# Prompt attention of a two-layer decoder trunk: softmax normalised on the finished output instead of on the probabilities

## What is computed

```python
def block(args):                      # one block of 128 queries
    qi, ci, pi = args
    s = jnp.einsum('bqhd,bkhd->bhqk', qi, k).astype(F32) * scale
    s = s + ci[..., None] - ckt[:, :, None, :]
    s = jnp.where(k_pos[None, :] <= pi[:, None], s, MASK_VALUE)
    p = jax.nn.softmax(s, axis=-1).astype(v.dtype)
    return jnp.einsum('bhqk,bkhd->bqhd', p, v)
```

## Time and profile before

| | us |
|---|---|
| median of three runs | 2067.57 (2066.80 to 2072.34) |
| the profiled execution, time | 2069.26 |
| the profiled execution, span of the trace | 2066.1 |
| TensorE busy in the span | 1897.4 (92%) |
| VectorE busy in the span | 920.6 (45%) |
| ScalarE busy in the span | 673.6 (33%) |
| first score product of prompt attention to the end of its last output copy | 1070.93 to 1169.36: 98.4 |

### The profile page before, as it was taken

The page is one execution under the profiler, slowest core; times in us unless marked ns, Lnnn a source line. Parts: engine busy times, 40 slices in busy tenths (PEclk is TensorE's granted clock), DMA queues, the critical chain, the costliest instruction groups (busy, mean ns, idle before and its releaser), DMA issues. The chain is left out here.

```text
span 2066.1 us, 39402 instructions
## 1 busy us (share of the span) xinstructions
PE 1897.4 (92%) x16433; PEld 1726.6 (84%) x16433; DVE 920.6 (45%) x1393; ACT 673.6 (33%) x1047; POOL 572.9 (28%) x263
## 2 busy tenths in 40 slices
PE   4999997999999999998979779888887999999998
PEld 4899996899999999998967546555546999999998
DVE  3767756235555400234448744433332255555100
ACT  4455464232222222344326424333332422222111
POOL 1333231233333433333335100000002333333332
PEclk9999998999999999999979979999997999999999
DMA  4232331222222322222231389999992222223222
GB/s 104 73 104 77 86 95 45 72 73 84 85 86 84 87 85 71 64 69 62 72 115 46 91 320 377 390 388 388 389 379 85 78 82 82 82 82 90 85 85 74
DMA packets 288994, 272.91 MB, mean 132 GB/s; under 512 B 19953, under 2 KB 249426, under 8 KB 288178
## 3 DMA queue, kind: packets, MB, share of 16 engines
q1 hardware_dynamic: 288674, 269.35, 40.3%
q0 software_dynamic: 144, 1.05, 0.2%
HBM read 252.09 MB, written 14.08 MB: 129 GB/s over the span
## 5 line engine op out<-in xcount | busy, mean ns | idle before, releaser
L1713 POOL TENSOR_TENSOR b_wl<-b_wraw,b_wh 128x1024 fp32r<-128x1024 f32 (+1 forms) x68 | 177.4, 2609 | 714.5 <-ACT b_wh L1651 714.5
L1713 POOL TENSOR_TENSOR a_wl<-a_wraw,a_wh 128x1024 fp32r<-128x1024 f32 (+2 forms) x91 | 243.3, 2674 | 433.3 <-ACT a_wh L1651 433.3
L1609 PE MATMUL ps<-xh,a_wh 128*128 128x288 f32 x1104 | 242.9, 302 | 0.0
L1609 PE MATMUL ps<-xl,a_wh 128*128 128x288 f32 x1104 | 238.0, 297 | 0.0
L1609 PE MATMUL ps<-xh,a_wl 128*128 128x288 f32 x1104 | 237.4, 297 | 0.0
L1651 ACT ACTIVATE a_wh<-a_wraw 128x1024 fp32r<-128x1024 f32 (+2 forms) x91 | 100.5, 1104 | 354.4 <-PE ps L1609 348.9
L1201 PEld LDWEIGHTS ps<-ident,sa_kp 128*128 128x128 f32 x1024 | 125.4, 154 | 83.9 <-DMA sa_kp<-in_cache_k 50.2
L1201 PE MATMUL ps<-ident,sa_kp 128*128 128x128 f32 x1024 | 141.8, 298 | 53.5 <-DMA sa_kp<-in_cache_k 44.3
L1651 ACT ACTIVATE b_wh<-b_wraw 128x1024 fp32r<-128x1024 f32 (+1 forms) x68 | 77.1, 1134 | 346.3 <-PE ps L1609 319.1
L1728 DVE TENSOR_TENSOR xT<-xT,ps 128x576 f32<-128x576 f32 x32 | 24.1, 754 | 355.3 <-PE ps L1609 355.3
L1609 PEld LDWEIGHTS ps<-xh,a_wh 128*128 128x128 f32 x1104 | 179.1, 188 | 3.0 <-issue 0.2
(11 more groups left out here) (296 smaller groups left out, 3872.6 us busy)
## 6 DMA issues: line engine op xcount, KB each, us to landing
sa_kp<-in_cache_k SPq DMA_DIRECT2D x128, 512.0 KB, 10.1
sa_vp<-in_cache_v SPq DMA_DIRECT2D x128, 512.0 KB, 14.5
a_wraw<-in_w_gate_up SPq DMA_DIRECT2D x44, 512.0 KB, 3.9
b_wraw<-in_w_gate_up SPq DMA_DIRECT2D x44, 512.0 KB, 3.9
a_wraw<-in_a_w_in SPq DMA_DIRECT2D x32, 512.0 KB, 4.1
a_wraw<-in_w_down SPq DMA_DIRECT2D x16, 704.0 KB, 4.6
b_wraw<-in_w_down SPq DMA_DIRECT2D x16, 704.0 KB, 4.6
a_wraw<-in_w_kvf SPq DMA_DIRECT2D x16, 512.0 KB, 4.1
```

Of the source, the lines that this page charges most:

```text
L1609: mm = pe.matmul(ps[0:width(n), bank(n) + a, 0:HALF], wt[:, base(n) + t, 0:width(n)], ap[:, first + t, a * HALF:(a + 1) * HALF], start=kin ...
L1713: pool.tensor_tensor(part(wl, n), part(wraw, n), part(wh, n).bitcast(F32), ALU.subtract).then_inc(e["low"], 1)
```

## The change

The scaling of the probabilities by VectorE is dropped, and with it the semaphore `scaled`. The reciprocals `inv` stay (`inverse`, L948 of the changed kernel). Transposes take the unscaled probabilities and wait for the exponential alone. After each `mix`, TensorE makes two more products: the column `inv` of a head, repeated over 64 columns, times the 128x128 identity (L849). That writes each query's inverse sum to all 64 partitions of its head, in bank 7 of PSUM, which the scores no longer use: they have three banks instead of four. When a pair is finished ScalarE copies bank 7 to a new buffer `whole` (`keep`, in the turn 3 of the next pair), and VectorE multiplies the pair's output by it into `oT` (`output`, in turn 4 of the next pair). ScalarE's copy of the output is dropped.

The lags change too: TensorE does `turn(w - 2)` instead of `turn(w - 3)` and, for odd `w`, `mix(w - 5)`. The copies on ScalarE and VectorE keep their lag of 3.

```diff
--- before.py
+++ after.py
@@ -755,13 +755,12 @@
 
 
     nc, ps = k.nc, k.ps
-    e = {n: k.sem("pa_" + n) for n in ("const", "rounded", "ones", "qhigh", "khigh", "qlow", "klow", "scored", "max", "exp", "inv", "scaled", "turned",
-                                       "mixed", "done")}
+    e = {n: k.sem("pa_" + n) for n in ("const", "rounded", "ones", "qhigh", "khigh", "qlow", "klow", "scored", "max", "exp", "inv", "turned", "mixed",
+                                       "spread", "kept", "done")}
     rows = [k.sem(f"pa_rows{a}") for a in range(2)]
     placed = [k.sem(f"pa_placed{s}") for s in range(2)]
     U, PLACES = 8, 6
-    PR, SC, PT = 4, 4, 4
-    SCORE_BANKS = (0, 1, 2, 7)
+    PR, SC, PT = 4, 3, 4
     N = KD * U
     with ExitStack() as st:
         sb = lambda n, shape, dt=F32: k.sb(st, "pa_" + n, shape, dt)
@@ -769,7 +768,7 @@
         qb, kb = (sb(n, [DH + 4, 2, 2, SEQ], F32R) for n in ("qb", "kb"))
         causal_r, ident_r = sb("causal_r", [P, P], F32R), sb("ident_r", [P, P], F32R)
         nm, tot, inv = (sb(n, [P, 8]) for n in ("nm", "tot", "inv"))
-        pr, pt = sb("pr", [P, PR, SEQ]), sb("pt", [P, PT, SEQ])
+        pr, pt, whole = sb("pr", [P, PR, SEQ]), sb("pt", [P, PT, SEQ]), sb("whole", [P, SEQ])
         causal = pr[:, 0, 0:P]
 
         def unit(w):
@@ -780,7 +779,7 @@
             return (w % U // 2 + 1) * P
 
         def score_bank(w):
-            return SCORE_BANKS[w % SC]
+            return w % SC
 
         with nc.Block() as block:
             @block.sync
@@ -823,7 +822,7 @@
                     pe.matmul(out, qb[:, s, a, i * P:(i + 1) * P], kb[:, s, a, 0:n], start=False, stop=True).then_inc(e["scored"], 1)
 
                 def turn(w):
-                    pe.wait_ge(e["scaled"], w + 1)
+                    pe.wait_ge(e["exp"], w + 1)
                     if w >= 2:
                         pe.wait_ge(rows[w % 2], w // 2)
                     for c in range(width(w) // P):
@@ -842,6 +841,13 @@
                             mm = pe.matmul(ps[DH * a:DH * (a + 1), 5 + j % 2, i * P:(i + 1) * P],
                                            vrows[:, c, (2 * j + a) * DH:(2 * j + a + 1) * DH], pt[:, (first + a) % PT, c * P:(c + 1) * P],
                                            start=c == 0, stop=c == i, skip_group_check=True)
+                    if i == 0 and j >= 1:
+                        pe.wait_ge(e["kept"], j)
+                    pe.wait_ge(e["inv"], first + 2)
+                    for a in range(2):
+                        s = (first + a) % 8
+                        mm = pe.matmul(ps[DH * a:DH * (a + 1), 7, i * P:(i + 1) * P], inv[:, s:s + 1].broadcast_to([P, DH]), k.ident[:],
+                                       start=True, stop=True, skip_group_check=True)
                     mm.then_inc(e["mixed"], 1)
 
                 pe.wait_ge(e["rounded"], 2)
@@ -849,10 +855,10 @@
                 for w in range(N + 6):
                     if w < N:
                         score(w)
-                    if 3 <= w < N + 3:
-                        turn(w - 3)
-                    if w >= 6 and w % 2 == 0:
-                        mix(w - 6)
+                    if 2 <= w < N + 2:
+                        turn(w - 2)
+                    if w % 2 == 1 and 0 <= w - 5 < N:
+                        mix(w - 5)
 
             @block.scalar
             def _(act):
@@ -879,9 +885,11 @@
                         act.wait_ge(e["mixed"], (w - PT) // 2 + 1)
                     act.activation(pt[:, w % PT, 0:n], ps[:, 3 + w % 2, 0:n], ACT.Copy).then_inc(rows[0], 1)
 
-                def output(j):
+                def keep(j):
                     act.wait_ge(e["mixed"], 4 * j + 4)
-                    act.activation(oT[:, j * T:j * T + SEQ], ps[:, 5 + j % 2, :], ACT.Copy).then_inc(e["done"], 1)
+                    if j > 0:
+                        act.wait_ge(e["done"], j)
+                    act.activation(whole[:], ps[:, 7, :], ACT.Copy).then_inc(e["kept"], 1)
 
                 for j in range(2):
                     for a in range(2):
@@ -897,8 +905,8 @@
                     j = w // U + 1
                     if w % U in (2, 4) and 2 <= j < KD:
                         query_high(j, w % U // 2 - 1)
-                    if w % U == 7 and w >= 2 * U - 1:
-                        output(w // U - 1)
+                    if w % U == 3 and w > U:
+                        keep(w // U - 1)
 
             @block.gpsimd
             def _(pool):
@@ -932,14 +940,16 @@
                         dve.wait_ge(e["exp"], w - 7)
                     dve.tensor_reduce(nm[:, s], ps[:, score_bank(w), 0:n], AX.X, ALU.max, negate=True).then_inc(e["max"], 1)
 
-                def scale(w):
-                    n, s = width(w), slice(w % 8, w % 8 + 1)
+                def inverse(w):
+                    s = slice(w % 8, w % 8 + 1)
                     dve.wait_ge(e["exp"], w + 1)
                     if w >= 8:
-                        dve.wait_ge(e["scaled"], w - 7)
+                        dve.wait_ge(e["mixed"], (w - 8) // 2 + 1)
                     dve.reciprocal(inv[:, s], tot[:, s]).then_inc(e["inv"], 1)
-                    dve.wait_ge(e["inv"], w + 1)
-                    dve.tensor_scalar(pr[:, w % PR, 0:n], pr[:, w % PR, 0:n], inv[:, s], None, ALU.mult).then_inc(e["scaled"], 1)
+
+                def output(j):
+                    dve.wait_ge(e["kept"], j + 1)
+                    dve.tensor_tensor(oT[:, j * T:j * T + SEQ], ps[:, 5 + j % 2, :], whole[:], ALU.mult).then_inc(e["done"], 1)
 
                 def copy(w):
                     n = width(w)
@@ -950,13 +960,15 @@
 
                 dve.memset(qb[DH:DH + 4].bitcast(F32), 1.0).then_inc(e["ones"], 1)
                 dve.memset(kb[DH:DH + 4].bitcast(F32), 1.0).then_inc(e["ones"], 1)
-                for w in range(N + 4):
+                for w in range(N + 8):
                     if w < N:
                         maximum(w)
                     if 1 <= w < N + 1:
-                        scale(w - 1)
-                    if w >= 4 and (w - 3) % 2 == 1:
+                        inverse(w - 1)
+                    if w >= 4 and (w - 3) % 2 == 1 and w - 3 < N:
                         copy(w - 3)
+                    if w % U == 4 and w > U:
+                        output(w // U - 1)
 
 
 class PastDecay:
```

## The result

The changed kernel takes 2073.56 us (median of 22 runs) against 2067.89 (22 runs of the kernel before). The ratio is 1.0024, with a 95% interval of 1.0016 to 1.0032: slower by 3 to 7 us, where 2083.5 was forecast (+16), with a range of 2075 to 2094. Two of the changed kernel's 22 runs, of 2165 and 3712 us, were slow ones and stand outside the ratio.

What follows compares the result with a forecast made beforehand. VectorE looked like the bound, tied to a DMA loop; after the change a copy-to-transposes loop takes 13.2 us a pair against 11.37. The stage sum +16.8, taken as +16, on the median 2067.57 gives 2083.5 us, range 2075 to 2094.

Steps and rivals of the forecast that it cites:

- each of the four laps: Loop over every two units, four a pair: TensorE stands 0.5, 1.0, 0.5 and 0.5 us for VectorE's part.
- VectorE's load: VectorE in the changed stage: busy about 60% and waiting for scores, its load down by 40%.
- four reciprocals until the next starts, 0.19: VectorE's reciprocals in the loop, each 0.19 us until the next instruction starts: 0.76 of 13.2 us a pair.
- Pair 3 with 6.9 us at 1.2 GHz: Fourth pair keeps its 6.9 us of low TensorE clock: 15.8 us against 13.61, +2.2.
- pair 7 plus 3.4 us: Last pair and tail, 17.9 us, plus 3.4 us at 1.2 GHz times 0.38: 19.2 against 17.07, +2.1.
- rival 2: TensorE's clock: 25 us more at 1.2 GHz gives 2093, both old stretches vanishing 2079.5; chance 0.15 together with dearer spread products.
- The 14 us at 1.2 GHz in pairs 0 and 1: Stage's start keeps 14 us of low TensorE clock: first two pairs 27.4 us against 22.13, +5.3.
- The difference of two stages added to the median: Stage change, taken as +16 against the profiled execution of 2069.26, added to the median 2067.57: 2083.5 us.
- Rival 1: VectorE delivers copies before transposes ask; TensorE's own work is 10.7 us a pair: 2067 to 2068, no change; chance 0.12.
- rival 4: Only the scaling mattered: copies don't bind and the clock stays at 2.4 GHz, 10.7 us a pair, 2059.5; chance 0.03.
- Rival 3: TensorE's spread products are dear, their weights not hidden: +8 on the forecast, 2091; chance 0.15 together with a dearer clock.
- The edits at no cost: Three score banks, ScalarE's `keep` (0.60 us, replacing the dropped copy) and VectorE's output product; only the last product counts.

Runs made afterwards that it cites:

- first experiment: Changed kernel with ScalarE and VectorE copying the turned probabilities of unit w - 2, not w - 3: 2062.93 us, ratio 0.9966 against the kernel before.
- third: Kernel before with only TensorE's lags shortened (turn of w - 2, mix of w - 5), VectorE's scaling and four score banks kept: 2080.33 us, ratio 1.0064.

## Why the prediction was wrong

**The mechanism was right in the main.** Pairs start 12.65 us apart at 2.4 GHz without a DMA wait, apart from one of 0.39 us; transposes wait for copies that kept the old lag; moving the copies too (first experiment) takes back the loss, and the lag alone (third) causes one. But TensorE's idle time, forecast for VectorE's copy in each of the four laps, stands ahead of VectorE's in two of them and ahead of ScalarE's in the other two, a way the prediction didn't have. VectorE's load, forecast at about 60%, was 53% (21.27 of 40 us).

**What failed is the size of two terms:** the reciprocals, and the low clock carried over. The forecast sum was +16.8 for the stages of the two traces; measured is +7.3:

| | forecast | measured |
|---|---|---|
| pairs 0 and 1 | +5.3 | +2.1 |
| pair 2 | +1.8 | +1.5 |
| pair 3 | +2.2 | -1.1 |
| pairs 4 to 6 | +5.4 | +3.7 |
| pair 7 | +2.1 | +1.1 |

- *The term "four reciprocals until the next starts, 0.19"* was read between the reciprocal and the scaling. The scaling waits for its own reciprocal; the copy behind it doesn't. In the changed kernel the copy starts 0.07 us behind the reciprocal (1135.31 to 1135.38). In four laps that is 0.48 of the 0.55 by which a pair was too long, 3.4 us over seven pairs. In the first lap ScalarE's copy took the 0.12 back (3.27 us measured, 3.3 forecast), so it may be nearer 0.36, 2.5 us. The row had the right instruction and the wrong successor: the first step that failed.
- *"Pair 3 with 6.9 us at 1.2 GHz" and "pair 7 plus 3.4 us"* carried the falls of before over to the changed kernel, where neither trace has one: 10.3 times 0.38, 3.9 us. The prediction had this as the lower end of rival 2 (2079.5), and had noted that each fall stood behind a DMA wait, and that the change removes those waits; it drew no conclusion from the two. That is the second step that failed: the low stretches were taken as given, and they come with waits that the change removes.
- *The 14 us at 1.2 GHz in pairs 0 and 1* were 10 in the changed kernel's first trace (to about 1079), 1.4 us. Over all the traces the first rise came 6.5 to 17.5 us behind the first score, with no rule that these runs show.
- *The difference of two stages added to the median.* The trace of before was one with few falls. The two stages of before are 98.4 and 105.3 us, those of the changed kernel 105.8 and 105.8: by the means +3.9, by the medians of all runs 5.7. The rest of the program, the same in all kernels, took 1964 to 1969 us in the 13 traces, and 3.5 us less in the changed kernel's first trace than in the first of before, so that the two traced executions differ by 2.5 us only. That the runs of before without a trace fall as often as these two is inferred, from the 22 runs' median and from the 8.8 us that the earlier queries alone gained.

**The rivals.** Rival 1 (the copies don't bind) and rival 4 fell with the waits for copies. Rival 3 fell with the doubled products. Rival 2 had the right subject: both old stretches vanished, its low end of 2079.5; what lies below that is the reciprocals' term and the start of the stage.

**The edits at no cost** held: three banks, `keep` and the output product show no wait in the changed kernel beyond ScalarE's 0.6 us ahead of `keep`, with exponential 4 on time, and the tail's 5.6 us (18.20 less 12.65) against 4.7.

## What to carry to other kernels

When an order by lags is shortened in one place, look for every wait that the lag was there to cover, on each engine that has a part in it: here it was a bank's reuse, released by copies that kept the old lag. The removed scalings alone gave 15 us and the lag alone cost 13 (both by the ratios); the new products, put at the 6.9 us by which doubling them lengthened the stage, make the estimated sum +5, near what was measured. Read a gap between two instructions together with what the second one waits for; once another follows, the gap is another. A stretch at a low clock can come with the kernel's waits: before carrying it over, ask whether what stands ahead of it is still there, and take two traces of the base.

## What was not expected of the hardware

TensorE fell from 2.4 to 1.2 GHz in or within 2 us behind waits ahead of a pair that left it idle for only 0.75 to 2.6 us, in 10 of 24 cases, and never in the stages without such waits. Gaps in mid-pair brought no fall, neither the changed kernel's four a pair, of 0.3 to 0.8 us, nor those of 1.1 us with the shorter lag alone. The time from the second query copy to the next pair's first score was 3.56 us as a rule, but 4.22 ahead of 1130.22 in the first trace of before (the copy starts at 1126.00) and 4.73 ahead of 1125.79 in the kernel with the later query (1121.06), with the same transfers; what delays them wasn't tried.
